# Five query and score steps of a PEER layer moved into the build of its gate matrix

## The chip, the cores and the metric

The kernel runs on one core of one Trainium2 chip, in float32. The metric is device time in microseconds. One profiled execution is read beside the timed runs. The engines are TensorE (PE; PEld for its weight loads), VectorE (DVE), ScalarE (ACT), GpSimd (POOL) and SyncE (SP, which only issues transfers).

## The reference

The model is one encoder block on x (1024 tokens x 1024). Two mixers (SSD and HGRN2) and their projections come first; the change doesn't touch them. Then comes `peer_ffn`, a product-key expert layer:

```python
q = (xt @ w_query).reshape(t, PEER_HEADS, 2, PEER_HALF)              # 8 heads, 2 halves of 128
s = jnp.einsum('thpd,hpnd->thpn', q, sub_keys)                       # scores of 128 keys per half
s_top, i_top = lax.top_k(s, PEER_TOPK)                               # 16 best of each half
cand = s_top[:, :, 0, :, None] + s_top[:, :, 1, None, :]             # 16 x 16 sums
c_top, c_idx = lax.top_k(cand, PEER_TOPK)                            # 16 best pairs -> expert, gate
expert = idx1 * PEER_KEYS + idx2                                     # 16384 experts
hid = gelu(einsum(x, u_table[expert])) * gate
out = einsum(hid, v_table[expert])                                   # summed over heads and experts
```

A residual add and a final RMSNorm follow.

## The kernel before, in words

`peer` is the last and longest part. The tokens lie in eight blocks of 128. The first four blocks are computed **densely**: all 16384 experts are multiplied for all their tokens, and a gate matrix, nearly all zeros, selects. The last four blocks are computed by **gathering**: for each token and head, the rows of the 16 chosen experts are fetched from `u_table` and `v_table` by indirect transfers.

**Units and steps.** A unit is one head of one block. Units 0 to 31 are of the dense blocks, 32 to 63 of the gathered ones. A step i makes the queries (`query`, L1793: 16 matmuls 128x256, in the profile 32 instructions, since a float32 matmul is recorded as two) and the key scores (`score`, L1803: 4 matmuls, 8 instructions) of units 2i and 2i + 1. ScalarE copies the queries out of PSUM (L1874) and the scores into `R.sc` (L1879), and then issues the loads of the next step's weights into `wk` (L2003, L2004). VectorE routes each unit: `route_keys` (L1150 to L1164), `route_pairs` (L1181 to L1191), `route_experts` and `route_gates` (L1195 to L1205). Step 16 (units 32, 33) is made before `peer`, in `mix_out`.

**The build.** 96 groups (`for j in range(M_GROUPS)`) build the gate matrix of three dense blocks, four tokens a group. VectorE makes one-hot tiles (`hot`, L2038 and L2042), ScalarE one more (`hot_last`, L1903, L1906), TensorE multiplies them (L1833), ScalarE copies the product into staging tiles (`place_out`, L1919, L1922), and SP stores the staging tiles to the DRAM tensor `sel`, in twelve halves, two after every 16 groups. All tiles are double-buffered. VectorE stops after groups 24 and 60 (`ROUTE_AT`) to route units 32 and 33.

**The loop.** 256 slots, in 16 loop groups of 16. In a group, slots 0 to 7 each compute the hidden values of 128 experts for the 512 dense tokens (L1852: 8 matmuls 128x512), and slots 8 to 15 each one output tile (L1865). ScalarE applies GELU (L1930) and VectorE multiplies by the gate tile (`dense`, L2054, in the slot after); in the output slots it adds the product to the sum (L2061). The first output slot needs all eight hidden tiles. Beside that, every slot handles two gathered rows per token: GpSimd issues gathers of u rows (L1761) and v rows (L1768) into rings of five, VectorE makes the dot products (`dot`, L2067) and adds the weighted v rows (`combine`, L2078). The last stores of `sel` must be complete before the first v gathers and before the first loads of gate tiles (`load_sel`, L1949).

A unit takes 8 slots (m = slot // 8, sl = slot % 8), so a loop group holds two. Unit DU + m + 2 (34 at first) is routed at sl 3, 5 and 7. Queries stand in TensorE's order by `next_query` and `score_at`: step 17 at slots 0 and 2, then one step in every odd m, at sl 0 and sl 4, that is in slots 8 and 12 of a loop group; steps 18 to 31 fill loop groups 0 to 13, and the last two have none.

Each engine works through its own instructions in program order; semaphores join them.

Of the kernel before, what the change touches and what calls it, by code (L numbers as in the profile page):

```python
# [59 lines left out]
OB = 3  # L60
SELB = 64
MB = DB - 1
PAIR = 2 * DB * P
LOW = -3.0e38

# [1077 lines left out]
    return n // 2 % PH  # L1143


def route_keys(nc, dve, own, R, n):
    dve.wait_ge(R.scores_out, n // 2 + 1)
    sc, top = R.sc[:, n % 2], R.ti[:, 0]
    for p in range(2):
        own.step(nc.vector.max(top[:, p, 0:8], sc[:, p, :]))  # L1150
    own.hold()
    for p in range(2):
        nc.vector.max_index(R.ix[:, p, 0:8], top[:, p, 0:8], sc[:, p, :])
        own.step(nc.vector.match_replace(R.sc2[:, p, :], top[:, p, 0:8], sc[:, p, :], LOW))
    own.hold()
    dve.sem_inc(R.picked, 1)
    for p in range(2):
        own.step(nc.vector.max(top[:, p, 8:16], R.sc2[:, p, :]))
    own.hold()
    for p in range(2):  # L1160
        ins = nc.vector.max_index(R.ix[:, p, 8:16], top[:, p, 8:16], R.sc2[:, p, :])
    own.now(ins)
    own.now(nc.vector.tensor_copy(R.ti[:, 1], R.ix[:]))
    own.now(nc.vector.tensor_scalar(R.ti[:, 1, 0, :], R.ti[:, 1, 0, :], float(KEYS), None, ALU.mult))  # L1164
# [426 lines left out]
            gate_of(DU - 1)  # L1591


def peer(nc, w_route, u_cols, v_cols, u_rows, v_rows, fin_w, sel, C, Y, hnT, R, out):

# [3 lines left out]
    with ExitStack() as ctx:  # L1599
# [60 lines left out]
        def m_tile(e):  # L1660
# [14 lines left out]
        f_squared, f_meaned, f_rooted, f_inverse, f_normed = (sem("f_squared"), sem("f_meaned"), sem("f_rooted"),  # L1675
                                                              sem("f_inverse"), sem("f_normed"))
        written, dve_own = sem("written"), sem("dve_own")
        od = out.rearrange("o (b p) d -> p (o b) d", p=P)
        block = ctx.enter_context(nc.Block())

# [1 line left out]
        PER_BATCH = SELB // 4  # L1682
        HALVES = 2 * MB * P // SELB
        LATE_PICKS = {40: 2}
        ROUTE_AT = (24, 60)
        END = PAIRS

        def sel_stores(i):
# [20 lines left out]
        FINISH_IN_LOOP = 2  # L1709
        TURN_AT = 2 * PH - 4  # L1710

        def next_query(m):

            if m == 0:
                return DS + 1
            i = DS + (m + 3) // 2
            return i if m % 2 == 1 and i < STEPS else None

        def score_at(m):

            return 2 if m == 0 else 4

        @block.sync
        def _(sp):
            sp.dma_start(wk[:, 0:WQ], w_route[1, :, 0:WQ]).then_inc(R.wq_in[1], 16)
            sp.dma_start(wk[:, WQ:WK], w_route[1, :, WQ:WK]).then_inc(R.keys_in[1], 16)
            for x in range(HALVES):
                batch, hh = x // 2, x % 2
                if x == HALVES - 2:
                    sp.wait_ge(pick_turned, MB)  # L1730
                    for e in range(UT):
                        sp.dma_start(ut[e], u_cols[e]).then_inc(u_in[e], 16)
                sp.wait_ge(staged, 2 * (PER_BATCH * (batch + 1) - 1) + hh + 1)
# [50 lines left out]

        @block.tensor
        def _(pe):
            def query(i):
                pe.wait_ge(R.wq_in[1], weights_in(i))
                need(pe, R.q_out, i)
                need(pe, x_out, 4 * ((i - DS) // PH))  # L1790
                for p in range(2):
                    for k in range(KT):
                        mm = nc.tensor.matmul(ps_q[:, p, :], wq[:, k, p * P:(p + 1) * P], xg[:, k, :],  # L1793
                                              start=(k == 0), stop=(k == KT - 1))
                mm.then_inc(R.q_made, 1)

            def score(i):
                pe.wait_ge(R.q_out, i + 1)
# [38 lines left out]
            for slot in range(PAIRS):  # L1837
                g, s = slot // SLOTS, slot % SLOTS
# [1 line left out]
                i = next_query(m)  # L1840
                if i is not None and sl == 0:
                    query(i)
                if i is not None and sl == score_at(m):
# [26 lines left out]
        def _(act):  # L1870
# [5 lines left out]
            def score_out(i):  # L1876
                act.wait_ge(R.scores_made, i + 1)
                act.wait_ge(R.picked, 2 * i)
                nc.scalar.activation(R.sc[:], ps_s[:], ACT.Copy).then_inc(R.scores_out, 1)  # L1879

            def gates(n):
                act.wait_ge(R.best_ready, n + 1)
# [91 lines left out]
            for j in range(M_GROUPS):  # L1974
# [5 lines left out]
                place_out(j, 1)  # L1980
                if j in ROUTE_AT:
                    gates(DU + ROUTE_AT.index(j))
            load_sel(0)
            load_sel(1)
            for slot in range(PAIRS):
# [9 lines left out]
                    x_copy(sl - 2)  # L1995
                if n < UNITS and sl == 5:
                    gates(n)
                if i is not None and sl == score_at(m) + (1 if m > 0 else 0):
                    score_out(i)
                if i is not None and sl == score_at(m) + 2:  # L2000
                    act.wait_ge(R.scores_made, i + 1)
                    if i + 1 < STEPS:
                        act.dma_start(wk[:, 0:WQ], w_route[(i + 1) % PH, :, 0:WQ]).then_inc(R.wq_in[1], 16)  # L2003
                        act.dma_start(wk[:, WQ:WK], w_route[(i + 1) % PH, :, WQ:WK]).then_inc(R.keys_in[1], 16)  # L2004
                    else:
                        act.dma_start(fw, fin_w).then_inc(fw_in, 16)
                if 1 <= s <= GE and s % 2 == 0 and g * GE + s + 2 < KEYS:
                    load_sel((g * GE + s + 2) // 2)
# [16 lines left out]
        def _(dve):  # L2025
# [86 lines left out]
            for slot in range(PAIRS + 1):  # L2112
# [27 lines left out]


def block_program(nc, x, ln_w, w_ssd, par, w_hg, lb_logits, w_out, mix_w, ffn_w, w_route, u_cols, v_cols, u_rows, v_rows,
                  fin_w, sel, out):
    with ExitStack() as ctx:
        C = {n: ctx.enter_context(nc.sbuf_tensor(n, [P, P], F32)) for n in ("ident", "ones", "tri", "below")}
        hnT = ctx.enter_context(nc.sbuf_tensor("hnT", [P, 2, KT, HALF], F32))
# [3 lines left out]
        sel_zeroed = ctx.enter_context(nc.semaphore("sel_zeroed"))  # L2150
        with nc.sbuf_tensor("reset", [P, SEQ], F32) as reset, nc.sbuf_tensor("lmask", [P, LEVELS + 1, P], F32) as lmask:
            C["reset"], C["lmask"] = reset, lmask
            with nc.sbuf_tensor("w_group", [P, KT, SSD_COLS], F32) as w_group, ExitStack() as held:
                group_in = [held.enter_context(nc.semaphore(f"group_in{i}")) for i in range(len(SSD_PARTS))]
                hw = held.enter_context(nc.sbuf_tensor("hw", [P, 2 * CT * (TAPS - 1 + HALF)], F32))
                H = Heads(nc, held, w_group[:], hw)
# [5 lines left out]
        peer(nc, w_route, u_cols, v_cols, u_rows, v_rows, fin_w, sel, C, Y, hnT, R, out)  # L2162


def laid_out(inputs):
# [56 lines left out]
```

## Time and profile before

| | |
|---|---|
| timed runs, median (lowest) | 3664.1 us (3662.92) |
| the profiled execution | 3663.56 us |
| its span, first to last instruction | 3661.8 us |
| mean granted TensorE clock | 0.975 |
| PE busy | 3457.3 us, 94% |
| DVE busy | 2862.0 us, 78% |
| ACT busy | 1059.2 us, 29% |
| POOL busy | 1436.1 us, 39% |
| chain that ended last, by line | L1865 24%, L1852 22%, L1793 2%, of the span |
| transferred | 829.66 MB, mean 227 GB/s |

"Busy" is the union of an engine's instruction times. "Idle before" names the instruction whose end released the waiting one. The build lies between 1581 and 1741 us of the span, the loop from 1741 to about 3642 us.

### The profile page before, as it was taken

What the parts mean: (1) busy time and instruction counts of PE and PEld (TensorE: products, weight loads), DVE (VectorE), ACT (ScalarE), POOL (GpSimd) and SP (SyncE); (2) the same over time, 40 slices, a digit from 0 to 9 for tenths busy, and PEclk for the clock granted to TensorE, in tenths of its full rate; (3) what the DMA queues carried; (4) which work ended last, traced back from release to release, by engine and by line L of the source; (5) the groups of instructions that cost most, each with busy time, mean ns of one, the idle gap of its engine ahead of it and who ended that gap; (6) DMA issues with size and microseconds to landing.
All of it is one profiled execution on the core that took longest, in us unless ns stands there. A gap on an engine that the chain in (4) does not pass through costs nothing.

```text
span 3661.8 us, 40046 instructions
## 1 busy us (share of the span) xinstructions
PE 3457.3 (94%) x11593; PEld 1984.5 (54%) x11593; DVE 2862.0 (78%) x6720; ACT 1059.2 (29%) x2649; POOL 1436.1 (39%) x1232
## 2 busy tenths in 40 slices
PE   7999989999997999667899999999999999999997
PEld 4666667777774565456444444444444444444443
DVE  2466676767783399889598889887898889888997
ACT  3233344444452222168111112111211122111211
POOL 1000000000001177500466666655666566665664
PEclk9999999999997999889999999999999999999999
DMA  3111022000103134236999999999999999999997
GB/s 110 29 35 35 0 73 66 23 29 29 34 0 135 51 64 83 34 108 182 374 386 373 398 389 382 378 387 356 388 374 388 387 393 378 376 392 377 390 382 293
DMA packets 313937, 829.66 MB, mean 227 GB/s; under 512 B 41504, under 2 KB 145056, under 8 KB 305056
## 3 DMA queue, kind: packets, MB, share of 16 engines
q0 software_dynamic: 165888, 537.01, 39.7%
q1 hardware_dynamic: 125104, 227.45, 17.1%
q10 hardware_dynamic: 22768, 63.18, 4.4%
q8 instruction: 69, 1.13, 0.1%
q14 instruction: 108, 0.88, 0.1%
HBM read 789.73 MB, written 37.81 MB: 226 GB/s over the span
## 4 chain that ended last, share of the span: by engine, by line
PE 48%; issue 4%; DVE 2%; DMA 1%; POOL 0%; ACT 0%; ACTq 0%; DVEq 0%; POOLq 0%
PE peer_ps_o L1865 24%; PE peer_ps_d L1852 22%; PE peer_ps_q L1793 2%; DMA peer_vr<-in_v_rows,peer_index 1%; DVE peer_mt L2038 0%; DVE peer_mt L2042 0%; DVE Y L2078 0%; DMA peer_ur<-in_u_rows,peer_index 0%; PE peer_ps_s L1803 0%; DVE Y L2095 0%; POOL peer_ur L1761 0%; POOL peer_vr L1768 0%; DVE peer_ur L2067 0%; PE peer_ps_o L1833 0%; DVE route_hit L1197 0%
## 5 line engine op out<-in xcount | busy, mean ns | idle before, releaser
L1761 POOL DMA_INDIRECT peer_ur<-in_u_rows,peer_index x512 | 563.7, 1101 | 613.3 <-DVE peer_ur L2067 401.3
L1768 POOL DMA_INDIRECT peer_vr<-in_v_rows,peer_index x512 | 599.5, 1171 | 321.8 <-issue 150.6
L2078 DVE SCALAR_TENSOR_TENSOR Y<-peer_vr,peer_hid,Y 128x1024 f32<-128x1024 f32 x512 | 657.0, 1283 | 82.1 <-DMA peer_vr<-in_v_rows,peer_index 82.0
L2067 DVE SCALAR_TENSOR_TENSOR peer_ur<-peer_ur,Y 128x1024 f32<-128x1024 f32 x512 | 627.5, 1226 | 10.9 <-DMA peer_ur<-in_u_rows,peer_index 9.9
L1852 PE MATMUL peer_ps_d<-hnT,route_ut 128*128 128x512 f32 x1376 | 598.5, 592 | 0.0
L1865 PE MATMUL peer_ps_o<-peer_va,Y 128*128 128x512 f32 x1024 | 446.1, 596 | 12.7 <-DVE Y L2054 12.7
L1865 PE MATMUL peer_ps_o<-hnT,Y 128*128 128x512 f32 x1024 | 442.1, 592 | 0.0
L1852 PEld LDWEIGHTS peer_ps_d<-hnT,route_ut 128*128 128x128 f32 x1376 | 261.3, 190 | 327.7 <-issue 327.7
L1865 PEld LDWEIGHTS peer_ps_o<-peer_va,Y 128*128 128x128 f32 x1024 | 195.4, 191 | 254.8 <-issue 236.1
L1865 PEld LDWEIGHTS peer_ps_o<-hnT,Y 128*128 128x128 f32 x1024 | 193.5, 190 | 238.2 <-issue 238.2
L1852 PE MATMUL peer_ps_d<-hnT,peer_ut 128*128 128x512 f32 x672 | 295.3, 592 | 0.0
L1937 ACT ACTIVATE peer_act_out<-peer_dots 128x2 f32<-128x2 f32 x256 | 51.3, 200 | 819.3 <-DVE peer_ur L2067 802.7
L1517 POOL DMA_INDIRECT sel<-route_ut,mo_sel_index x128 | 211.8, 1654 | 170.5 <-DVE route_ut L1205 112.4
L1930 ACT ACTIVATE Y<-peer_ps_d 128x512 f32<-128x512 f32 x128 | 76.3, 596 | 683.1 <-PE peer_ps_d L1852 665.2
L512 PE MATMUL ssd_ps_piece<-hnT,w_group 128*128 128x512 f32 x512 | 228.0, 598 | 6.9 <-ACT hw L595 5.1
L1503 POOL IOTA mo_count_u<- 128x128 uint32 x1 | 0.2, 239 | 595.9 <-POOLq L808 595.9
L1361 PE MATMUL mo_ps_h<-mo_w,mo_yT 128*128 128x512 f32 x512 | 228.1, 604 | 1.1 <-DVE Y L1572 1.1
L1852 PEld LDWEIGHTS peer_ps_d<-hnT,peer_ut 128*128 128x128 f32 x672 | 127.4, 190 | 159.3 <-issue 159.3
L494 POOL TENSOR_TENSOR ssd_awide<-ssd_a,tri 128x512 f32<-128x512 f32 x32 | 34.5, 1077 | 451.4 <-PE ssd_ps_rows L556 404.3
L894 PE MATMUL hg_ps_piece<-hnT,hw 128*128 128x512 f32 x448 | 199.2, 598 | 6.4 <-ACT hg_raw_vg L953 6.4
L898 PE MATMUL hg_ps_piece<-hw,hnT 128*128 128x256 f32 x896 | 198.0, 379 | 0.0
L898 PEld LDWEIGHTS hg_ps_piece<-hw,hnT 128*128 128x128 f32 x896 | 168.1, 190 | 21.7
(320 smaller groups left out, 4935.6 us busy)
## 6 DMA issues: line engine op xcount, KB each, us to landing
route_ut<-in_u_cols SPq DMA_DIRECT2D x86, 512.0 KB
peer_va<-in_v_cols SPq DMA_DIRECT2D x16, 2048.0 KB
peer_mt<-sel ACTq DMA_DIRECT2D x64, 512.0 KB
hnT<-in_v_cols SPq DMA_DIRECT2D x16, 2048.0 KB
peer_ut<-in_u_cols SPq DMA_DIRECT2D x42, 512.0 KB
route_wk<-in_w_route ACTq DMA_DIRECT2D x14, 1024.0 KB
hnT<-in_w_route SPq DMA_DIRECT2D x9, 1024.0 KB
route_wk<-in_w_route SPq DMA_DIRECT2D x9, 1024.0 KB
```

The lines of the kernel that those rows point to most:

```text
L512: mm = nc.tensor.matmul(bank, w[:, k, i * P:(i + 1) * P], hnT[:, half, k, :], start=(k == 0), stop=(k == KT - 1))
L894: mm = nc.tensor.matmul(bank, w[:, kt, p * P:(p + 1) * P], hnT[:, half, kt, :], start=(kt == 0), stop=(kt == KT - 1))
L898: mm = nc.tensor.matmul(bank[:, 0:2 * P], hnT[:, half, kt, cols(p - 2)], w[:, kt, 2 * P:4 * P], start=(kt == 0), stop=(kt == KT - 1))
L1361: mm = nc.tensor.matmul(ps_h[:, half, :], yT[:, k, :], w[:, k, half * 512:(half + 1) * 512], start=(k == 0), stop=(k == MT - 1))
L1517: pool.indirect_dma_start(sel.rearrange("a i q two (t o) -> (a i q two t) o", o=1), bass.IndirectOffsetOnAxis(ap=sel_index[:, h, k:k + 1], ...
L1761: pool.indirect_dma_start(ur[:, r % RING, :], None, u_rows, bass.IndirectOffsetOnAxis(ap=index[:, r // TOPK % 4, r % TOPK:r % TOPK + 1], a ...
L1768: pool.indirect_dma_start(vr[:, r % RING, :], None, v_rows, bass.IndirectOffsetOnAxis(ap=index[:, r // TOPK % 4, r % TOPK:r % TOPK + 1], a ...
L1852: mm = nc.tensor.matmul(ps_d[:, e % 2, :], ut[e % UT][:, k, :], xT[:, k, :], start=(k == 0), stop=(k == KT - 1))
L1865: mm = nc.tensor.matmul(ps_o[:, o % OB, :], ht(e, tb), v_tile(e, half), start=(j == 0), stop=(j == GE - 1))
L1930: nc.scalar.activation(ht(e), ps_d[:, e % 2, :], ACT.Gelu).then_inc(gelu_done, 1)
L2067: nc.vector.scalar_tensor_tensor(out=ur[:, s, :], in0=ur[:, s, :], scalar=1.0, in1=Y[:, b, D:MIX], op0=ALU.mult, op1=ALU.mult, accum_out=d ...
L2078: nc.vector.scalar_tensor_tensor(out=hb, in0=vr[:, s, :], scalar=hid[:, c:c + 1], in1=hb, op0=ALU.mult, op1=ALU.add).then_inc(comb_done, 1)
```

## The change

Steps 17 to 21 (`AHEAD = 5`) are made during the build. In groups 9 to 16 TensorE issues two of the step's 16 query matmuls after each group's own; ScalarE copies the queries out at the next group, TensorE scores at the one after, and ScalarE then issues the next step's weight loads, copies the scores into half of `ut2` and stores them to a DRAM tensor `held`. The next step starts 16 groups after the one before (9, 25, 41, 57, 73). SP waits for all five stores before it loads the first u_cols tiles. In the loop ScalarE loads held scores into `R.sc` in place of the query, the score and the copy; from step 22 on everything is as before. Unit 33 is routed in loop slots 0 to 2, no longer in the build.

```diff
+AHEAD = 5
-def route_keys(nc, dve, own, R, n):
-    dve.wait_ge(R.scores_out, n // 2 + 1)
+def route_keys(nc, dve, own, R, n, held_in=None):
+    if held_in is None:
+        dve.wait_ge(R.scores_out, n // 2 + 1)
+    else:
+        dve.wait_ge(held_in, 16 * (n // 2 - DS))
...
-        ROUTE_AT = (24, 60)
+        ROUTE_AT = (24,)
...
+        def step_of(m):
             i = DS + (m + 3) // 2
             return i if m % 2 == 1 and i < STEPS else None
+        def next_query(m):
+            i = step_of(m)
+            return i if i is not None and i > DS + AHEAD else None
+        def next_held(m):
+            i = step_of(m)
+            return i if i is not None and i <= DS + AHEAD else None
+        def held_place(i):
+            return ut2[:].rearrange("p k c -> p (k c)")[:, i % 2 * 4 * KEYS:(i % 2 + 1) * 4 * KEYS]
+        SCORE_AT = 4
+        START, SCORED = 9, KT + 1
+        def ahead(j):
+            k, at = (j - START) // BATCH, (j - START) % BATCH     # BATCH = 16
+            return (DS + 1 + k, at) if 0 <= k < AHEAD else (None, -1)
...
         # SP, before the first u_cols loads (half store 10 of 12)
                     sp.wait_ge(pick_turned, MB)
+                    sp.wait_ge(held_out, 16 * AHEAD)
...
         # TensorE, after the matmuls of build group j
                 mm.then_inc(sel_made, 1)
+                step, at = ahead(j)
+                if 0 <= at < KT:
+                    query(step, [2 * at, 2 * at + 1])
+                if at == SCORED:
+                    score(step)
...
         # ScalarE
+            def hold_scores(i):
+                k = i - DS - 1
+                act.wait_ge(R.scores_made, i + 1)
+                need(act, held_out, 16 * (k - 1))
+                nc.scalar.activation(held_place(i)..., ps_s[:], ACT.Copy).then_inc(R.scores_out, 1)
+                act.wait_ge(R.scores_out, i + 1)
+                act.dma_start(held[k], held_place(i)).then_inc(held_out, 16)
+            def load_weights(i):
+                act.wait_ge(R.scores_made, i)
+                act.dma_start(wk[:, 0:WQ], w_route[i % PH, :, 0:WQ]).then_inc(R.wq_in[1], 16)
+                act.dma_start(wk[:, WQ:WK], w_route[i % PH, :, WQ:WK]).then_inc(R.keys_in[1], 16)
+            def load_held(i):
+                act.wait_ge(R.picked, 2 * i)
+                act.wait_ge(held_out, 16 * AHEAD)
+                act.dma_start(R.sc[:]..., held[i - DS - 1]).then_inc(held_in, 16)
         # ScalarE, at the end of build group j
+                step, at = ahead(j)
+                if at == KT:
+                    query_out(step)
+                if at == SCORED + 1:
+                    load_weights(step + 1)
+                    hold_scores(step)
         # ScalarE, in the loop
+                if slot == 1:
+                    gates(DU + 1)
+                    load_held(DS + 1)
+                if next_held(m) is not None and sl == SCORE_AT + 1:
+                    load_held(next_held(m))
...
         # VectorE, in the loop
+                if slot == 0:
+                    route_keys(nc, dve, own, R, DU + 1)
+                if slot == 1:
+                    route_pairs(nc, dve, own, R, DU + 1)
+                if slot == 2:
+                    experts(DU + 1)
                 if n < UNITS and sl == 3:
-                    route_keys(nc, dve, own, R, n)
+                    route_keys(nc, dve, own, R, n, held_in if n // 2 <= DS + AHEAD else None)
```

## Rows read from the trace of the kernel before

**Rows 1.** Chain of waits in order, loop group 3: start us, us, work.

```profile
2114.53 54.93 PE peer_ps_d L1852 x128
2169.47 6.91 PE peer_ps_q L1793 x32
2176.37 27.47 PE peer_ps_o L1865 x64
2203.84 0.89 PE peer_ps_s L1803 x8
```

**Rows 2.** VectorE timeline, same group: start, us, instruction, [idle before <- releaser].

```profile
2164.97 1.28 DVE L2078 SCALAR_TENSOR_TENSOR Y<-peer_vr,peer_hid,Y 128x1024 f32<-128x1024 f32 x1 [3.13 <-DMA peer_vr<-in_v_rows,peer_index]
...
2177.53 0.68 DVE L2054 TENSOR_TENSOR Y<-Y,peer_mt 128x512 f32<-128x512 f32 x1
```

**Rows 3.** Timeline at the loop's start, then VectorE's waits, 1768 to 1827 us.

```profile
1767.98 0.69 DVE L2054 TENSOR_TENSOR Y<-Y,peer_mt 128x512 f32<-128x512 f32 x1 [26.18 <-issue]
...
1826.94 0.68 DVE L2054 TENSOR_TENSOR Y<-Y,peer_mt 128x512 f32<-128x512 f32 x1
...
1827.68 2.93 PE L1865 MATMUL peer_ps_o<-peer_va,Y 128*128 128x512 f32 x3 [7.91 <-DVE Y L2054]
...
DVE Y L2078 <- DMA peer_vr<-in_v_rows,peer_index: 7.4, 4, 3.2
```

**Rows 4.** Build groups: timeline, then a window (PE, PEld, DVE, ACT, POOL busy).

```profile
1599.23 1.13 PE L1833 MATMUL peer_ps_o<-peer_mt 128*128 128x128 f32 x8 [0.25 <-DVE peer_mt L2042]
...
1616.04 1.13 PE L1833 MATMUL peer_ps_o<-peer_mt 128*128 128x128 f32 x8 [0.24 <-DVE peer_mt L2042]
...
1700.00:1720.00 20.00, 15.96 (x115) 13.59 (x113) 20.00 (x58) 19.50 (x58) 0.00 (x0) 1.00 0.62 176
```

**Rows 5.** Timeline around the route of unit 33 in the build.

```profile
1680.47 1.13 PE L1833 MATMUL peer_ps_o<-peer_mt 128*128 128x128 f32 x8 [0.30 <-DVE peer_mt L2042]
...
1683.68 0.54 DVE L1181 TENSOR_TENSOR route_ce<-route_ti 128x32 f32<-128x32 f32 x5
...
1689.48 0.68 DVE L2038 TENSOR_TENSOR peer_mt<-route_count,peer_pickedT 128x512 f32<-128x512 f32 x1
...
1694.75 1.13 PE L1833 MATMUL peer_ps_o<-peer_mt 128*128 128x128 f32 x8 [0.25 <-DVE peer_mt L2042]
```

**Rows 6.** One line (min/median/max ns); ScalarE after three transfer issues.

```profile
L1874 ACT ACTIVATE route_qs<-peer_ps_q x15: 572/574/576, 1762.3 to 3370.7; 128x512 f32<-128x512 f32 x15
...
1796.34 0.60 ACT L1930 ACTIVATE Y<-peer_ps_d 128x512 f32<-128x512 f32 x1 [0.91 <-issue]
```

**Rows 7.** Transfers (last number: us to landing); one issue and wait.

```profile
sel<-hnT SPq DMA_DIRECT2D x3, 2048.0 KB, 15.2
...
w_group<-in_w_ssd SPq DMA_DIRECT2D x4, 1040.0 KB, 5.6
...
1794.95 0.37 ACTq L2003 DMA_DIRECT2D route_wk<-in_w_route  x1
...
1805.28 7.17 PE L1793 MATMUL peer_ps_q<-route_xg,route_wk 128*128 128x256 f32 x32
...
  DMA route_wk<-in_w_route: 0.8, 1
```

**Rows 8.** Chain of waits, the loop group without a query; windows after its stall.

```profile
3416.71 20.61 PE peer_ps_d L1852 x48
...
3481.41 50.89 PE peer_ps_o L1865 x114
3532.30 54.93 PE peer_ps_d L1852 x128
...
3482.00:3488.00 6.00, 6.00 (x12) 2.50 (x11) 6.00 (x10) 0.68 (x3) 3.32 (x3) 0.72 1.02 416
```

**Rows 9.** Windows, loop group 3; last columns: clock, DMA share, GB/s.

```profile
2116.00:2124.00 8.00, 8.00 (x20) 3.61 (x19) 7.93 (x15) 1.17 (x4) 4.20 (x4) 1.00 0.90 316
...
2148.00:2156.00 8.00, 8.00 (x21) 3.46 (x20) 7.96 (x16) 1.40 (x5) 3.75 (x4) 1.00 1.03 415
```

More of the change, by code:

```diff
@@ L1591, in _, with peer @@
             gate_of(DU - 1)
-def peer(nc, w_route, u_cols, v_cols, u_rows, v_rows, fin_w, sel, C, Y, hnT, R, out):
+def peer(nc, w_route, u_cols, v_cols, u_rows, v_rows, fin_w, sel, held, C, Y, hnT, R, out):
     with ExitStack() as ctx:
@@ L1677, in peer @@
         written, dve_own = sem("written"), sem("dve_own")
+        held_out, held_in = sem("held_out"), sem("held_in")
         od = out.rearrange("o (b p) d -> p (o b) d", p=P)
@@ L1710, in peer @@
         TURN_AT = 2 * PH - 4
-        def next_query(m):
-            if m == 0:
-                return DS + 1
+        def step_of(m):
             i = DS + (m + 3) // 2
             return i if m % 2 == 1 and i < STEPS else None
-        def score_at(m):
-            return 2 if m == 0 else 4
+        def next_query(m):
[7 more added lines that the diff above has]
+        SCORE_AT = 4
+        BATCH = SELB // 4
+        START, SCORED = 9, KT + 1
+        def ahead(j):
+            k, at = (j - START) // BATCH, (j - START) % BATCH
+            return (DS + 1 + k, at) if 0 <= k < AHEAD else (None, -1)
         @block.sync
@@ L1786, in _, with query @@
         def _(pe):
[L1787 to L1795, printed above, removed]
+            def query(i, parts=range(2 * KT)):
+                if parts[0] == 0:
+                    pe.wait_ge(R.wq_in[1], weights_in(i))
+                    need(pe, R.q_out, i)
+                    need(pe, x_out, 4 * ((i - DS) // PH))
+                for part in parts:
+                    p, k = part // KT, part % KT
+                    mm = nc.tensor.matmul(ps_q[:, p, :], wq[:, k, p * P:(p + 1) * P], xg[:, k, :],
+                                          start=(k == 0), stop=(k == KT - 1))
+                if parts[-1] == 2 * KT - 1:
+                    mm.then_inc(R.q_made, 1)
             def score(i):
@@ L1842, in _ @@
                     query(i)
-                if i is not None and sl == score_at(m):
+                if i is not None and sl == SCORE_AT:
                     score(i)
@@ L1879, in score_out @@
                 nc.scalar.activation(R.sc[:], ps_s[:], ACT.Copy).then_inc(R.scores_out, 1)
+            def hold_scores(i):
+                k = i - DS - 1
+                act.wait_ge(R.scores_made, i + 1)
+                need(act, held_out, 16 * (k - 1))
+                nc.scalar.activation(held_place(i).rearrange("p (j q c) -> p j q c", j=2, q=2), ps_s[:],
+                                     ACT.Copy).then_inc(R.scores_out, 1)
+                act.wait_ge(R.scores_out, i + 1)
[7 more added lines that the diff above has]
+                act.wait_ge(held_out, 16 * AHEAD)
+                act.dma_start(R.sc[:].rearrange("p j q c -> p (j q c)"), held[i - DS - 1]).then_inc(held_in, 16)
             def gates(n):
@@ L1997, in _ @@
                     gates(n)
-                if i is not None and sl == score_at(m) + (1 if m > 0 else 0):
+                if i is not None and sl == SCORE_AT + 1:
                     score_out(i)
-                if i is not None and sl == score_at(m) + 2:
-                    act.wait_ge(R.scores_made, i + 1)
+                if slot == 1:
[3 more added lines that the diff above has]
+                    load_held(next_held(m))
+                if i is not None and sl == SCORE_AT + 2:
                     if i + 1 < STEPS:
-                        act.dma_start(wk[:, 0:WQ], w_route[(i + 1) % PH, :, 0:WQ]).then_inc(R.wq_in[1], 16)
-                        act.dma_start(wk[:, WQ:WK], w_route[(i + 1) % PH, :, WQ:WK]).then_inc(R.keys_in[1], 16)
+                        load_weights(i + 1)
                     else:
+                        act.wait_ge(R.scores_made, i + 1)
                         act.dma_start(fw, fin_w).then_inc(fw_in, 16)
@@ L2142, in block_program @@
 def block_program(nc, x, ln_w, w_ssd, par, w_hg, lb_logits, w_out, mix_w, ffn_w, w_route, u_cols, v_cols, u_rows, v_rows,
-                  fin_w, sel, out):
+                  fin_w, sel, held, out):
     with ExitStack() as ctx:
@@ L2152, in block_program @@
             C["reset"], C["lmask"] = reset, lmask
[L2153 to L2156, printed above, removed]
+            with nc.sbuf_tensor("w_group", [P, KT, SSD_COLS], F32) as w_group, ExitStack() as outer:
+                group_in = [outer.enter_context(nc.semaphore(f"group_in{i}")) for i in range(len(SSD_PARTS))]
+                hw = outer.enter_context(nc.sbuf_tensor("hw", [P, 2 * CT * (TAPS - 1 + HALF)], F32))
+                H = Heads(nc, outer, w_group[:], hw)
                 spent = input_norm(nc, x, ln_w, w_ssd, C, hnT, w_group, group_in)
@@ L2161, in block_program @@
         mix_out(nc, x, w_out, mix_w, ffn_w, w_route, sel, sel_zeroed, C, Y, osq, ysq, hnT, R)
-        peer(nc, w_route, u_cols, v_cols, u_rows, v_rows, fin_w, sel, C, Y, hnT, R, out)
+        peer(nc, w_route, u_cols, v_cols, u_rows, v_rows, fin_w, sel, held, C, Y, hnT, R, out)
 def laid_out(inputs):
@@ L2218 @@
     sel = nc.dram_tensor("sel", [KEYS, KEYS // 2, DB * P // SELB, 2, SELB], F32).ap()
-    block_program(nc, sel=sel, out=out, **args)
+    held = nc.dram_tensor("held", [AHEAD, P, 4 * KEYS], F32).ap()
+    block_program(nc, sel=sel, held=held, out=out, **args)
     r = run_bass_kernel_spmd(nc, [{"in_" + n: a for n, a in arrays.items()}], core_ids=[0])
```

## The prediction

> **What bounds the kernel now.** I read the page first: of the chain that ended last, TensorE's two dense lines hold 46% of the span and the query line 2% (the table above). So the loop is TensorE's; what leaves its stream there can be worth its full time, and no more. A change of 2% (73 us) is about what a measurement of this kernel can tell from none, and five steps are far less. I therefore looked for what each small term becomes at three places.
>
> *A loop group* takes, by the chain of waits, 54.93 us for eight scoring slots, 6.91 for a query, 27.47 + 0.89 + 27.47 for eight output slots with the score between: 117.67 [rows 1]. No stall is in it, so 7.80 us a step is the ceiling. But VectorE stands close behind. The first output slot's eighth matmul needs the eighth hidden tile, ready at 2177.53 + 0.68 = 2178.2, which is 63.7 us after the group's start at 2114.53 [rows 1, 2]. TensorE wants it seven matmuls (7 x 0.859 = 6.0 us) after the query, at 2182.4. The reader is to see that these 4.2 us of slack exist only because the query stands there; and that VectorE's way to that tile holds a wait of 3.13 us for a gathered row [rows 2], which the change doesn't touch.
>
> *The start* hangs on the last stores of the gate matrix. VectorE's slot 1 begins at 1767.98 after 26.18 us of idleness, its hidden tile 8 is ready at 1826.94 + 0.68, and TensorE, which already made the query of step 18, had to wait for it, the last time 7.91 us [rows 3].
>
> *The build* runs at (1616.04 - 1599.23) / 12 = 1.40 us a group. TensorE works 1.13 of it and idles 0.25, while in 20 us VectorE is busy 20.00 and ScalarE 19.50 [rows 4].
>
> **The change, part by part.**
>
> *The route of unit 33 leaves the build.* TensorE's last group before it starts at 1680.47, the third after it at 1694.75; three periods of 1.40 would put that at 1684.67 [rows 5]. Gain 10.1 us.
>
> *Query matmuls in the build*, beside 40 groups. Streamed, a gate group costs 0.89 (a score is the same eight 128x128 instructions) and two query matmuls 6.91 / 8 = 0.86 [rows 1]: 1.75 instead of 1.40, TensorE now the slowest, so 8 x 0.35 = 2.8 us a step. I take this because VectorE and ScalarE, double-buffered and then the faster ones, have the next operands ready. If the present gap stayed, 1.13 + 0.25 + 0.86 = 2.24, or 6.7 us a step.
>
> *The score and ScalarE's share*, per step. The score's 0.89 falls partly into gaps: 0.35. ScalarE has no slack, so the copy of the queries (0.574 [rows 6]) costs 0.45 after overlap. Then come two weight issues, the copy of the scores (same size) into the held place, the wait for its own completion, one more issue. Three issues in the loop left ScalarE 0.91 idle [rows 6]; with the copy and the wait 1.6 us. Sum 2.8 + 0.35 + 0.45 + 1.6 = 5.2 a step, 26 for five. Low end 12 (2.4 a step: both engines catch up on their part while TensorE is the slow one); high end 51 (6.7 + 0.89 + 0.57 + 2.1 = 10.3 a step).
>
> *Weights in time?* They are issued at the step's 11th group and wanted six groups later, some 8.5 us. A load of 1040 KB landed in 5.6 us without company; one issued at 1794.95 with all queues full held up TensorE's query by 0.8 us until 1805.28, so it took 10.3 [rows 7]. In the build only the stores share the engines. I take 1.5 us in all (0 to 9: up to 3 on each of three steps; the first is covered by the route after group 24).
>
> SP's wait for all five held stores moves the first u_cols loads from group 80 to about 85. Ten groups, 14 us, are left for them, and TensorE then reaches slot 1's end early and stands until ScalarE, itself waiting for the stores, gives it free. Nothing; if that cover failed, the last stores, queued behind on SP, and all after them would move by the overrun.
>
> *Start of the loop.* Queries 17 and 18 vanish from a stretch where TensorE waits anyway: nothing. VectorE gets unit 33: route_keys in slot 0, inside its 26.18 us of idleness, and pairs and experts in slots 1 and 2, 5.8 us (1683.68 to 1689.48 [rows 5]). Before hidden tile 8 it waits for v gathers alone for 7.4 us [rows 3]. The engines of the transfers are full there and lose 1.18 MB of weights but get twice 0.26 of held scores, 1.6 us at 415 GB/s. Net +1 us (-2 to +5.8). The table loads for slot 1's exponent delay the third GELU, which the query's vanished 6.9 us cover. The score of step 18 stands on the path: -0.9.
>
> *Loop groups 1 to 3* lose 7.80 us each, and TensorE wants the eighth tile at 54.93 + 6.01 = 60.94 but gets it at 63.7: it stalls 2.8. The trace has such a group, the one without a query: begun at 3416.71, TensorE wanted the tile at 3477.65 and went on at 3481.41, and the next group began at 3532.30. That is 115.59, a gain of 2.08 only [rows 8]. Part is the clock: after 3.8 us of idleness it was granted 0.72 on the mean of 6 us, a mix of 1.2 and 2.4 GHz, and 114 instructions took 50.89 instead of 48.9. My stall is shorter by a quarter; of these 2.0 us I take 1.0. Gain 7.80 - 2.76 - 1.0 = 4.05 a group, 12.1 for three; bounds 3 x 2.08 = 6.2 and 3 x 7.80 = 23.4. The Trainium skill, "TensorE: Matmul & The Clock Gate", section on HAM oscillation, warns that a gap in each round of a loop throttles the array anew each time; taken so, every such group pays the full 2.0 and the sum is 3 us higher.
>
> Can the transfers follow? A group moves 64 gathers and 22 other half-megabyte pieces, with the weights 45.2 MB; without them and with a held block 44.3, in 113.6 us 390 GB/s. A window of such a group shows 415 [rows 9]. The Trainium skill, "DMA: Bandwidth & Descriptors", section "Where 436 GB/s comes from", puts the HBM side at about 358 GB/s a core; by it no group could be as short as it is, so here the trace disagrees. Held scores are fetched six slots ahead: nothing.
>
> **Sum.** 26 + 1.5 - 10.1 + 1 - 0.9 - 12.1 = +5.4 us on the profiled execution's 3663.56: 3669.0 (the runs' median is 0.5 above it).
>
> **Rivals.**
> *A, the forecast*: build and loop nearly cancel; 3655 to 3682. 0.46.
> *B, cheap build and full gain in the loop*: 12 - 10.1 + 1 - 0.9 - 23.4 = -21.4: 3642. For it: TensorE idles in every build group [rows 4]. Against: the group of [rows 8]. 0.21.
> *C, slower: the gap stays.* Its place is the step from a query pair back to the gate matmuls; 51 instead of 26, sum +30.4: 3694. The kernel is slower as soon as a step costs over (10.1 + 0.9 + 12.1 - 2.5) / 5 = 4.1 us; over 2% would need 18.7, for which no row speaks. 0.20.
> *D, weights late*: served behind the stores, 2 MB of which took 15.2 us to land [rows 7], 6.5 us late on three steps: 18 more, 3687. 0.06.
> *E, no gain in groups 1 to 3, the transfers binding.* For it the DMA share of 1.03, against it other stretches with 0.90 and 316 GB/s [rows 9]. Sum +17.5: 3681. 0.04. The page's 358 GB/s would bring this about.
> The rest, 0.03, is unlisted.
>
> **Numbers.** 3645 to 3694 holds A, B's upper half, D, E and C up to its centre, some 0.8. Faster by over 2% 0.01, slower by over 2% 0.02, within 0.97.
>
> **What would show it.** Build: gate groups 1.75 us apart beside query pairs with TensorE busy throughout (C: 2.2), and the build 17 us longer. Loop: hidden tile 8 as long after the build as before; three groups of 113.6, each with one stall in the first output slot that VectorE's L2054 ends; the fifth group at 117.67 as before. Wrong if groups 1 to 3 don't stall there, if they stall over 4 us, or if waits for route weights or held scores stand high in the list of waits.

## The result, and the profile after

The median after is 3681.0 us (3677.3 to 3686.0), the ratio to the kernel before 1.0046, 95% interval [1.0034, 1.0058]: 0.3% to 0.6% slower, inside the range, inside "within 2%", and 1 us below the upper end of case A. One run of the kernel before, of 8221 us, and a later one of 8755 us were slow and are left out of every comparison. The medians lie 16.9 us apart, where the forecast was +5.4: direction and range were right, the forecast size was a third of what came. The profiled execution, the fastest of the five, took 3677.31 us with a span of 3675.6, 13.8 above the span before. The sum over the stretches:

| stretch | forecast | trace |
|---|---|---|
| up to the build's first group | 0 | -1.1 |
| build, first to last group (155.6 before) | +17.4 | +28.3 (183.9) |
| last group of the build to hidden tile 8 | +1 | -1.9 |
| the rest of loop group 0 | -0.9 | -0.5 |
| loop groups 1 to 3 | -12.1 | -8.9 |
| loop group 14, no query in either kernel | 0 | -2.2 |

The remaining 0.1 lies in the other loop groups.

**The build.** TensorE's timeline in a stretch with query pairs (start, us, instruction), the answer to [rows 4]:

```profile
1700.13 1.03 PE L1817 MATMUL peer_ps_q<-route_xg,route_wk 128*128 128x256 f32 x4
1700.99 1.05 PE L1858 MATMUL peer_ps_o<-peer_mt 128*128 128x128 f32 x8
1701.88 1.03 PE L1817 MATMUL peer_ps_q<-route_xg,route_wk 128*128 128x256 f32 x4
1702.75 1.05 PE L1858 MATMUL peer_ps_o<-peer_mt 128*128 128x128 f32 x8
...
1713.29 2.14 PE L1858 MATMUL peer_ps_o<-peer_mt 128*128 128x128 f32 x16
```

The gate groups from 1700.99 to 1713.29 are seven periods of 1.757 us, no line shows an idle time, and the forecast was 1.75. Then comes the end of a step, in the order of time:

```profile
1746.08 1.16 PE L1828 MATMUL peer_ps_s<-route_wk,route_qs 128*128 128x128 f32 x8 [0.96 <-ACT route_qs L1904]
...
1748.88 0.34 ACTq L1923 DMA_DIRECT2D route_wk<-in_w_route  x1
1749.25 1.16 ACTq L1924 DMA_DIRECT2D route_wk<-in_w_route  x1
...
1750.51 0.60 ACT L1916 ACTIVATE peer_ut<-peer_ps_s 128x512 f32<-128x512 f32 x1 [0.87 <-issue]
...
1751.13 0.49 ACTq L1919 DMA_DIRECT2D held<-peer_ut  x1
...
1751.67 0.38 ACT L1969 ACTIVATE Y<-peer_ps_o 128x256 f32<-128x256 f32 x1 [0.57 <-ACT peer_ut L1916]
...
1753.29 4.79 PE L1858 MATMUL peer_ps_o<-peer_mt 128*128 128x128 f32 x24 [2.35 <-ACT peer_vr L1972]
...
1754.63 0.69 DVE L2098 TENSOR_TENSOR peer_mt<-route_count,peer_pickedT 128x512 f32<-128x512 f32 x1 [2.12 <-PE peer_ps_o L1858]
...
1758.37 1.13 PE L1858 MATMUL peer_ps_o<-peer_mt 128*128 128x128 f32 x8 [0.29 <-DVE peer_mt L2102]
```

The reader is to see two holes in TensorE's row. The score waits 0.96 us for ScalarE's copy of the queries. Later a gate matmul waits 2.35 us, because ScalarE issued two loads, copied the scores, issued the store, and only then copied out the products that this matmul wants to overwrite. Issues don't count as busy: the 0.57 of idle time before that copy-out is the store's issue of 0.49 and 0.08 for all else, the wait for ScalarE's own copy included. And a slow TensorE hands the delay on: VectorE, the busiest engine of the build before, stands 2.12 us until TensorE gives a tile free. Over the whole build (engine, line, what it waited for: us in total, times, longest):

```profile
PE peer_ps_o L1858 <- DVE peer_mt L2102: 17.4, 20, 9.6
PE peer_ps_o L1858 <- ACT peer_vr L1972: 7.1, 3, 2.4
PE peer_ps_s L1828 <- ACT route_qs L1904: 4.9, 5, 1.0
PE peer_ps_o L1858 <- ACT hnT L1972: 4.7, 2, 2.4
...
DVE peer_mt L2098 <- PE peer_ps_o L1858: 34.6, 53, 3.0
```

The three waits of TensorE for ScalarE are 16.7 us for five steps. No wait for weights is in the list. The last line is the new one: in the kernel before VectorE waited 2.2 us for TensorE in the same window. After the second hole comes the clock (window; busy time of PE, PEld, DVE, ACT, POOL; granted clock, DMA share, GB/s):

```profile
1754.00:1758.00 4.00, 3.88 (x20) 3.49 (x19) 2.66 (x8) 3.17 (x10) 0.00 (x0) 0.57 0.99 374
```

**The loop.** The chain of waits (start, us, work), where [rows 1] had one unbroken stream in every group:

```profile
1903.93 20.61 PE peer_ps_d L1882 x48
...
1967.96 50.89 PE peer_ps_o L1895 x114
2018.85 20.61 PE peer_ps_d L1882 x48
...
2083.54 51.73 PE peer_ps_o L1895 x114
2135.27 20.61 PE peer_ps_d L1882 x48
...
2194.48 0.98 DVE route_hit L1199
2195.48 1.07 DVE route_hit L1201
2196.57 1.06 DVE peer_chosen L1203
2198.82 49.19 PE peer_ps_o L1895 x114
2248.01 54.93 PE peer_ps_d L1882 x128
```

Groups 1 to 3 take 114.92, 116.42 and 112.74 us, where 113.6 was forecast for each. TensorE wants tile 8 at 60.94 us after the group's start and goes on at 64.03, 64.69 and 63.55. So it stalls 3.1, 3.8 and 2.6 us (forecast 2.8) in the first output slot; group 4 is at 117.67 again. Three lines of VectorE's routing (`experts`) stand right before the tile: b_late below uses that. The same 114 instructions take 50.89, 51.73 and 49.19 us, by the clock behind the stall:

```profile
1970.00:1976.00 6.00, 6.00 (x12) 2.54 (x11) 6.00 (x9) 0.68 (x3) 4.29 (x4) 0.78 1.03 412
2085.00:2091.00 6.00, 6.00 (x11) 2.39 (x10) 6.00 (x8) 0.68 (x3) 3.90 (x3) 0.69 1.03 409
2201.00:2207.00 6.00, 6.00 (x15) 2.66 (x14) 6.00 (x9) 0.69 (x3) 4.29 (x4) 1.00 1.03 411
```

### The profile page after: what moved, and what is told of

It is laid out like the page before. It is cut to its first block, busy times and chain, and to the rows that moved or that the text cites. A ratio compares the mean times of both kernels' runs of the same rounds, so it can differ in the third digit from the quotient of the medians.

```text
span 3675.6 us, 40064 instructions
## 1 busy us (share of the span) xinstructions
PE 3460.3 (94%) x11593; PEld 1991.5 (54%) x11593; DVE 2863.6 (78%) x6720; ACT 1066.7 (29%) x2651; POOL 1436.7 (39%) x1232
## 4 chain that ended last, share of the span: by engine, by line
PE 47%; DVE 4%; DMA 3%; issue 2%; ACT 1%; POOL 0%; ACTq 0%; SPq 0%; DVEq 0%; POOLq 0%
PE peer_ps_o L1895 23%; PE peer_ps_d L1882 19%; PE peer_ps_q L1817 3%; DMA peer_vr<-in_v_rows,peer_index 2%; PE peer_ps_o L1858 2%; DVE Y L2138 1%; DVE peer_ur L2127 1%; PE peer_ps_s L1828 0%; DMA sel<-peer_vr 0%; DVE peer_mt L2102 0%; DVE peer_mt L2098 0%; DVE Y L2155 0%; DMA peer_mt<-sel 0%; DVE route_hit L1201 0%; DVE peer_chosen L1203 0%
## 6 DMA issues: line engine op xcount, KB each, us to landing
peer_va<-in_v_cols SPq DMA_DIRECT2D x16, 2048.0 KB, 10.6
```

## The experiments

Each was timed in turn with the kernel before, whose median was 3664.8 to 3665.2 us each time. T is my theory as it stood then.

### The loop's part alone: a_loop_only

```diff
 # the kernel before; in the loop, steps 19 to 21:
-                    query(i)          # and score(i), query_out(i), score_out(i)
+                    pe.sem_inc(R.q_made, 1)    # and so on: the semaphores alone
```

> The kernel before, with the query, the score and their two copies of steps 19 to 21 left out of the loop (the scores of step 18 are routed again; the weight loads and everything else stay). It gives the loop's part of the change alone. Theory T (VectorE's eighth hidden tile is late, TensorE stalls about 3 us in the first output slot and may lose up to 2.8 us more to the half clock): groups 1 to 3 take 113 to 116 us instead of 117.67, together 6 to 10 us less, 3655 to 3659. Rival R1 (TensorE's time is worth its full price in the loop, the build ate it): 7.8 us a group, 3641. Rival R2 (the transfers bind; here all weights are still loaded): no gain, 3664.

Measured: 3656.8 us, ratio 0.9976 [0.9967, 0.9985]; 8.4 below before. T holds: leaving three steps out of the loop altogether gives 2.8 us each, not the 7.8 that they occupy, and not nothing. The profiled run, among the slowest of its eleven, shows 5.5 us of it in groups 1 to 3. With the 10.1 of the route, the build must then have lost about 16.9 + 8.4 + 10.1 = 35.

### Parts of the build's price: f_two_of_16, d_pool, k_score_later

```diff
 # f: the changed kernel, query() in the build
+                    if len(parts) == 2 and k < KT - 1:
+                        continue
```

> The changed kernel with 2 of each step's 16 query matmuls in the build left out of the others' company: only the last two (of k = 7) are made, 14 are left out, so the scores of steps 17 to 21 mean nothing; weight loads, copies, scores and the held store stay. Theory T (the query matmuls beside the gate matmuls cost TensorE 0.35 us a group, 2.8 a step, and ScalarE's part of 4 to 5 us a step stands beside that): 7 of 8 pairs leave, 5 x 7 x 0.35 = 12 us, so 3669. Rival R1 (ScalarE has to do the same work in any case and catches up while TensorE is slow, so without the matmuls its part costs more): 3673 to 3678. Rival R2 (the query matmuls are the whole of the 38 us): 3650.

This kernel leaves out 14 of each step's 16 query matmuls, seven pairs' worth. Measured: 3669.0 us, ratio 1.0011 [1.0002, 1.0020]; 12.0 below the changed kernel, T's number. In its trace the build takes 170.1 us where the changed one takes 183.9: 2.76 less a step for seven pairs, 0.39 a pair where 0.35 was forecast, and so 3.15 for all eight. And 170.1 is still 23.7 above the build without the route and without moved steps (146.4 in the trace of i_route_only, below): 4.7 us a step, of which one pair takes 0.3 to 0.4. **Some 4.4 us a step stand there without any of these matmuls**, where the forecast had 2.4.

```diff
 # d: the changed kernel; the ten weight loads and five held stores of the build
-                    load_weights(step + 1)       # ScalarE
+            def keep(i):                         # GpSimd, idle there
+                pool.wait_ge(R.scores_made, i + 1)
+                pool.dma_start(wk[:, 0:WQ], ...); pool.dma_start(wk[:, WQ:WK], ...)
+                pool.wait_ge(R.scores_out, i + 1)
+                pool.dma_start(held[i - DS - 1], held_place(i)).then_inc(held_out, 16)
```

> The changed kernel, with the 15 transfers of the build (weights of the next step, held scores) issued by GpSimd instead of ScalarE; the copies stay on ScalarE. Nothing is left out. Theory S (ScalarE's 2.1 us halt for issues and its own completion makes TensorE idle 2.4 us and then run 4 us at half clock, once a step): the halt shrinks to the 0.6 us of the copy, TensorE's idle time to under 1 us; 2 us a step, 10 in all, 3671. Rival Q (the build's extra time is the query matmuls and the wait of the score for the copied queries): 0 to 3 us less, 3678 to 3681.

Measured: 3667.9 us, ratio 1.0007 [0.9998, 1.0016]; 13.1 below the changed kernel, 3 more than expected. The waits of its build:

```profile
PE peer_ps_s L1841 <- ACT route_qs L1917: 4.8, 5, 1.0
PE peer_ps_q L1830 <- DMA route_wk<-in_w_route: 3.6, 3, 1.9
PE peer_ps_o L1871 <- ACT peer_vr L1983: 2.8, 6, 0.7
PE peer_ps_o L1871 <- ACT hnT L1983: 1.6, 3, 0.7
...
DVE peer_mt L2108 <- PE peer_ps_o L1871: 24.5, 49, 2.4
```

The 11.8 us of gate matmuls waiting for ScalarE have become 4.4, and the build is 173.2 us long, 10.7 shorter. The mean granted clock of the whole build is 0.96 where it is 0.89 in the changed kernel, so a part of the gain is clock; how large a part isn't taken from the rest here. Now queries wait for weights, 3.6 us: a wait that the slower build had hidden. For step 19, say, the changed kernel issued the first load at 1658.52 and began the query at 1669.90, 11.4 us later and without a wait; here it is 10.6 us (1654.98 to 1665.62) with a wait of 1.26.

```diff
 # k: the changed kernel
-        START, SCORED = 9, KT + 1
+        START, SCORED = 9, KT + 2
```

> The changed kernel with each score in the build one group later (the second group after the last pair of query matmuls, not the first), so that ScalarE's copy of the queries has a whole group more; the next step's weights are issued a group later with it, still five groups before they are wanted. In the changed kernel's build the score waits for that copy five times, 4.9 us in all. Theory T (that wait stands on the path): the build 4 to 5 us shorter, 3676 to 3677, and the weights cost at most 1 us a step, 3676 to 3680. Rival R1 (ScalarE is behind in any case; the wait only moves to the gate matmul that waits for ScalarE, now 2.4 us a step and then 3.3): 3681. Rival R2 (the weights come late): 3683 or more, with waits for them in the trace.

Measured: 3672.9 us, ratio 1.0024 [1.0015, 1.0033]; 8.2 below the changed kernel, below T's range by 3. The score's wait is gone; what TensorE waits for otherwise in the build, and VectorE's wait:

```profile
PE peer_ps_o L1858 <- ACT peer_vr L1972: 8.4, 7, 2.6
PE peer_ps_o L1858 <- ACT hnT L1972: 5.3, 4, 2.4
PE peer_ps_q L1817 <- DMA route_wk<-in_w_route: 1.9, 2, 1.1
...
DVE peer_mt L2098 <- PE peer_ps_o L1858: 28.1, 52, 3.0
```

The build takes 175.9 us, 7.9 less than the changed one. Its waits for ScalarE are 1.9 us more (13.7 for 11.8), those for weights 1.9 more; with the 4.9 gone that explains 1.1. VectorE's row explains the rest: it waits 6.5 us less for TensorE (28.1 for 34.6) and 1.3 less of a kind without a releaser (0.9 for 2.2), together 7.8. So the wait stood on the path, and each microsecond of it cost more than itself. The clock that falls behind such holes is one likely part (0.91 on the mean of the build, for 0.89), but I did not take this apart.

### The loop's stall: b_late, c_fill

```diff
 # b: the changed kernel, VectorE in the loop
-                if n < UNITS and sl == 7:
-                    experts(n)
+                if m > 0 and n - 1 < UNITS and sl == 0:     # after the slot's own work
+                    experts(n - 1)
```

> The changed kernel, with VectorE's experts step of each unit moved from the end of slot 7 of its unit to the end of the next unit's slot 0, so behind the hidden tile that the first output slot needs. Nothing is left out. T: the tile comes 3.7 us earlier, at 60.0 us of its group, before TensorE wants it (60.9): no stall and no clock loss in groups 1 to 3 and 14, each near 110 us; 15 us from the three, 3 to 5 from the fourteenth, 3 to 4 at the loop's start. 3681 - 23 = 3658, and the runs, 3677 to 3686 now, lie within 3 us. R2 (transfers, or VectorE's whole work, bind): the stall only moves to a later slot, 3675 or more.

Measured: 3666.7 us, ratio 1.0008 [0.9999, 1.0017]; 14.3 below the changed kernel, but 23 were expected: halfway between T's 3658 and R2's 3675. The direction is right, the size was not: groups 1 to 3 take 113.1 us each (114.7 before the edit), not near 110. Their chain still has stalls of 1.3, 4.4 and 1.0 us:

```profile
1898.82 20.61 PE peer_ps_d L1882 x48
...
2075.59 51.49 PE peer_ps_o L1895 x114
2127.09 20.61 PE peer_ps_d L1882 x48
...
2188.98 49.19 PE peer_ps_o L1895 x114
2238.17 54.93 PE peer_ps_d L1882 x128
```

With `experts` out of the way the tile hangs on the gathered rows. In group 2, with the longest stall, VectorE is busy 105.8 us of 115.1 and waits 8.0 for them: it is itself nearly the bound, so R2 holds in part. Of the 12.0 us between the two profiled spans, 4.7 are in groups 1 to 3, 3.5 at the loop's start, 2.2 from group 14 on, and 1.4 ahead of the build, where the edit changes nothing.

```diff
 # c: the changed kernel, TensorE, ahead of the first output slot of groups 1 to 3
+                if s == GE and g in (1, 2, 3):
+                    for k in range(7):
+                        nc.tensor.matmul(ps_q[:, 0, :], xT[:, k, 0:P], xT[:, k, 0:2 * P], start=True, stop=True)
```

> The changed kernel, with seven useless 128x256 matmuls (3.0 us) for TensorE ahead of the first output slot of loop groups 1 to 3, where it stalls. Nothing is left out. T with its clock part: the stall is filled, the tile comes when it did, and the half clock behind the stall (0 to 2.8 us a group) is gone: 1.5 to 2 us a group less, 3676, with a smaller spread between runs. Without the clock part (the idle time alone costs): unchanged, 3681. If TensorE's time counted in full: 9 us more, 3690.

Measured: 3676.7 us, ratio 1.0036 [1.0024, 1.0048]; 4.3 below the changed kernel, as T had it. The two intervals overlap, so the medians alone wouldn't show this gain; the traces do, with 340.6 us for groups 1 to 3 where the changed kernel takes 344.1. The runs didn't move closer together, as T also had it (9.6 us from lowest to highest, 8.7 without the edit). Seven useless matmuls inside each stall, and the groups are faster, since all three now run their 114 instructions at the full clock:

```profile
1967.80 49.19 PE peer_ps_o L1898 x114
2081.72 49.19 PE peer_ps_o L1898 x114
2194.94 49.19 PE peer_ps_o L1898 x114
```

The stall itself is not shorter. This parts the two terms of the forecast: the stall, and the half-speed clock behind it.

### The cheap part of the change, and the better kernel: i_route_only, j_route_late, e_before_late

```diff
 # i: the kernel before
-        ROUTE_AT = (24, 60)
+        ROUTE_AT = (24,)
+                if slot == 0:                    # VectorE; gates(DU + 1) on ScalarE at slot 1
+                    route_keys(nc, dve, own, R, DU + 1)
+                if slot == 1:
+                    route_pairs(nc, dve, own, R, DU + 1)
+                if slot == 2:
+                    experts(DU + 1)
```

> The kernel before with the one cheap part of the change alone: unit 33 is routed by VectorE in loop slots 0 to 2 instead of after build group 60; no query or score is moved. Theory T (the route's 10.1 us leave the build whole, VectorE does them at the loop's start inside idle time but for a few us before hidden tile 8): -10.1 + 1 to 2, so 3655 to 3657, ratio 0.9975. Rival R1 (the loop's start swallows the gain, since the stores of the gate matrix and not the build's length set when slot 1's gate tile arrives): 3664, ratio 1.000. The last build group should start at 1729.5 and hidden tile 8's first reader at 1817 to 1819.

Measured: 3654.6 us, ratio 0.9975 [0.9965, 0.9984]; 10.2 below before, as T had it. In the trace the build takes 146.4 us, 9.2 less than before. The last build group starts at 1729.0, and from there to loop group 1 it is 140.3 us, 139.6 before: the start swallows 0.7, forecast 1. Group 14, which the edit doesn't touch, is 2.5 us shorter in this trace. So the changed kernel, 3681.0, is 26.4 us above its own cheap part.

The kernel j is i with the edit of b_late.

> The kernel of i_route_only with the experts of each unit made at the end of the next unit's slot 0, behind the eighth hidden tile, instead of at the end of slot 7, ahead of it. Theory T: the groups with a query do not wait for that tile (4.2 us of slack), so only the loop's start (some 2 us) and group 14, which has no query and stalls 3.8 us, gain: 2 to 5 us below i_route_only, so 3651 to 3654. Rival R1 (VectorE is the second bound in every group, and the order gains in all): 1 us a group, 15 us below. Rival R2 (late expert indices delay the gathers): slower than i_route_only by 5 us or more.

Measured: 3645.1 us, ratio 0.9948 [0.9933, 0.9962]; **the best of all**, 19.7 below before, and 9.5 below i, more than T's 2 to 5. Its profiled span is only 4.5 below that of i, 2.5 of it up to loop group 1 and 2.3 in group 14; but i's ten runs lie between 3651.0 and 3657.4, the profiled one lowest, j's five between 3643.9 and 3646.6, the profiled one highest. What i's other runs lose cannot be seen in one trace. R1's 15 us is out, as the groups with a query stay at 117.67 in j.

The kernel e is the kernel before with that edit alone.

> The kernel before with the experts of each unit made at the end of the next unit's slot 0, behind the eighth hidden tile, instead of at the end of slot 7, ahead of it; nothing else. Beside the routing moved to the loop the same edit gave 9.5 us. Theory T (it acts on the loop's start and on group 14's stall, with the clock that such a stall may cost): the same here, 3655 to 3659. Rival R1 (most of that gain came from unit 33's experts at slot 2 no longer meeting others at slot 7): 1 to 4 us only, 3661 to 3664. The groups with a query should keep 117.67 us each, group 14 fall from 115.59 to 111.

Measured: 3657.7 us, ratio 0.9981 [0.9972, 0.9990]; 7.2 below before. T holds, and group 14 doesn't stall any more in the trace; the two edits add (10.2 + 7.2 = 17.4, against 19.7).

### Does moving the steps pay with every cure? g_late_pool, l_all_cures, j_again

The kernel g has the edits of d and b, the kernel l those of d, b and k; j_again is j once more.

> The changed kernel with both cures together: the build's 15 transfers (ten weight loads, five stores of held scores) issued by GpSimd instead of ScalarE, and the experts of each unit made behind the eighth hidden tile. They act in different places, the build and the loop. Theory T: they add, 13.1 + 14.3 = 27 below the changed kernel, 3654, and 10 below the kernel before. Rival R1 (they share a gain, the start of the loop): 3658 to 3661. If T holds, the change with its two mis-sized terms mended is a small gain, and the best of the four.

Measured: 3655.3 us, ratio 0.9976 [0.9967, 0.9985]; 25.7 below the changed kernel, near T's 27: the two cures add up. But j, with the same route and the same late `experts` and all steps left in the loop, ran beside it with 3645.1: **the five moved steps cost 10.2 us even so.**

> The changed kernel with all three cures: transfers of the build issued by GpSimd, the experts of each unit behind the eighth hidden tile, and each score of the build one group later. Theory T (the score's wait for the query copy, 1.0 us five times, is still in the build of the kernel with two cures, but without ScalarE's issues less clock is lost with it): 4 to 6 us below g_late_pool's 3655.3, so 3649 to 3651, some 4 to 6 above j_route_late's 3645.1: moving the five steps is still no gain on top of the cheap part. Rival R1 (the cures overlap): 3655. Rival R2 (as the score alone did, 8 us): 3647, and with the clock kept 3645 or less, so that moving the steps pays.

> The kernel of j_route_late once more (the kernel before, unit 33 routed in the loop, experts made behind the eighth hidden tile), to stand on the same chip as l_all_cures. Both theories: 3645 to 3647. If l_all_cures lies above it by more than 3 us, the five steps cost more in the build than they give in the loop in spite of all cures.

Measured: l 3657.8 us, ratio 0.9980 [0.9971, 0.9989]; j_again 3647.0, ratio 0.9942 [0.9929, 0.9956]. T and R2 fell for l. R1, no further gain, had 3655, and l minus j_again is 10.8 us where g minus j was 10.2: the third cure, worth 8 alone, gives nothing here. A likely reason stands in its build:

```profile
PE peer_ps_q L1830 <- DMA route_wk<-in_w_route: 8.1, 3, 3.2
```

With the score a group later the loads are issued a group later too, and the weights are late three times by up to 3.2 us, 8.1 in all, for 3.2 in all in g's trace. That is rival D of the prediction on a smaller scale, though not in the changed kernel. But this trace is of l's slowest run, 3664.3, so it shows where such a run loses time and not what the median run did. The steps cost 10.2 us in g and 10.8 in l, the two best forms that I found for them.

## Why the prediction was right, and where it was not

**What held.** The query term: 2.8 a step, 2.9 by the period and 3.15 by f_two_of_16. The period of 1.75 us, and with it the end of rival C's mechanism: no gap stays beside the pairs. The route: 10.1, measured 9.2 in the build and 10.2 on the median of the whole kernel. Where the loop stalls, who ends the stall and about how long. Rival B's full gain is out (a_loop_only: 8.4 for three steps), rival E too: groups of 112.7 and 113.1 us have been run, at 409 to 412 GB/s after the stall, so the transfers do not bind at 117.67. That E's sum, 3681, is the measured time is luck: its mechanism isn't there.

**What failed.** The prediction's own sign for the build, 17 us longer, didn't come: it was 28.3. The step that failed is "the score and ScalarE's share", 0.35 + 0.45 + 1.6 = 2.4 us a step; it is about 4.5. A moved step costs the build 7.5 us in all ((183.9 - 146.4) / 5), halfway between the 5.2 of the forecast and the 10.3 of rival C. Of the 10.9 us by which the build exceeds the forecast, the steps are 11.5 and the smaller gain of the route 0.9, less the 1.5 for late weights that did not come. Two things were wrong in the step.
First, the 1.6 for three issues. It took ScalarE's idle time of 0.91 from the loop [rows 6]. There the second load's issue is short; in the build it isn't (shortest, median and longest of 14, in ns; the loop's take 450, the five of the build 1137 to 1167):

```profile
L1924 ACTq DMA_DIRECT2D route_wk<-in_w_route x14: 450/451/1167, 1617.2 to 3306.7; - x14
```

Why it takes longer there is not shown. ScalarE's idle time becomes 0.87 + 0.57 = 1.44, and with the copy of 0.60 the hole is 2.0 us, from 1749.64 to 1751.67, not 1.6. What it costs is more than its length, as TensorE stands 2.35 us because of it, then has a granted clock of 0.57 on the mean of 1754 to 1758, and VectorE, without slack, waits for TensorE. The prediction priced the hole by ScalarE alone. d_pool gives the loss, 10.7 us of the build, 2.1 a step for the issues alone, with the copies still on ScalarE.
Second, I costed the score as work (0.89, partly into gaps) and not as a wait. It asks one group after the last pair for a copy that ScalarE makes behind its own group's work, and stands 1.0 us five times. Moving it by one group makes the build 7.9 us shorter, 1.6 a step where 0.35 stood. The copies were not tried alone; if the two cures added, 0.8 a step would be left for them, but l_all_cures says that they don't simply add.

**The loop's gain** was 12.1 and came out as 8.9. The stalls sum to 9.5 (8.3 forecast); the clock took 1.7, 2.5 and 0 above 49.19, together 4.2, and 49.19 is itself 0.3 above the 48.9 of the undisturbed stream, three times, so that the forecast's 3.0 for the clock stands against 5.1: 23.4 - 9.5 - 4.2 - 0.9 = 8.8. The Trainium skill, "TensorE: Matmul & The Clock Gate", section on HAM oscillation, tells of waits in each round of a loop, long enough for it, that throttle the array anew each time. Read as the prediction took it, for every such group, the third should pay too. The trace disagrees for that one: after 2.6 us of idleness the granted clock stayed 1.00 and the 114 instructions took 49.19, while after 3.1 and 3.8 us it was 0.78 and 0.69. The stall's duration alone doesn't decide, as groups 2 and 3 of d_pool show (its chain of waits):

```profile
2010.10 20.61 PE peer_ps_d L1895 x48
...
2074.24 49.19 PE peer_ps_o L1908 x114
2123.43 20.61 PE peer_ps_d L1895 x48
...
2187.56 50.89 PE peer_ps_o L1908 x114
```

TensorE wants the tile at 60.94 us in both and goes on at 64.14 and 64.13, after a stall of 3.2 us; the first pays nothing and the second 1.7. What does decide is not shown.

**The start** gained 1.9 instead of losing 1. The kernel i, with the route there alone, loses 0.7. So the rest, some 2.6, comes with the moved steps, where the prediction took nothing for steps 17 and 18. Other traces agree: from the last build group to hidden tile 8 it is 86.0 to 86.3 us with moved steps (the changed kernel, c, d, f, k) and 88.1 to 88.7 without (the kernel before, a, i). What of the moved steps does it I did not take apart. **Group 14** gained 2.2 though nothing in it was changed: it stalled 3.2 us for 3.8, and its 114 instructions took 49.19 and not the 50.89 of [rows 8]:

```profile
3432.41 20.61 PE peer_ps_d L1882 x48
...
3496.58 49.19 PE peer_ps_o L1895 x114
```

One profiled run has 2 us more or less of this kind, and a sum that is read to 5 us must allow for it.

## What to carry to other kernels

Work moved into a "gap" is priced not by the engine that does it but by all that it hangs on the slower engines: here some 3 us a step on TensorE came with about 4.5 of ScalarE's copies, issues and waits, against a gain of 3 for each of three steps in the loop. Before moving a step, leave it out where it is: 8.4 us for three steps was all there was to win in that order of work, and two of the five stood where TensorE waits anyway. And when a change bundles edits, time each alone: the smallest of these (ten microseconds of VectorE's work moved into idle time) and a reordering of one routing step behind a tile that another engine wants gave 20 us, where the bundle lost 17.

## What the runs showed of the hardware that was not expected

- Of two weight loads issued back to back by ScalarE, the first took 0.34 us of its queue and the second 1.16 (1749.25), while the same second load took 0.45 in the loop; with the issues on GpSimd, which idles there, the gate matmuls' waits for ScalarE fell from 11.8 us to 4.4.
- The same stall may or may not cost half-speed clock after it: of two stalls of 3.2 us in one run (d_pool) one cost 0 and the other 1.7 us. With 7 useless matmuls in each of three stalls, the three groups together are 3.5 us shorter.
- Runs of one kernel lie up to 11 us apart (g: 3650.6 to 3661.9 in eleven, before: 3658.9 to 3668.4 in 25), those of j within 2.6 in the first series of five, and from 3641.0 to 3648.0 in the second. So differences below 3 us were not read from medians here.
